# Splitting the first projection of a two-block transformer kernel at half of its features, so that part of it runs between the modulation sums

## The reference

```
mod = silu(c) @ w_mod + b_mod                     # 1024 -> 3 x 1024
shift, scale, gate = split(mod, 3)
h = rms_norm(x, pre_gain) * (1 + scale) + shift   # 512 x 1024
proj = h @ w_in                                   # 1024 -> 3088 columns
```

## Time and profile before

| | us |
|---|---|
| median of 3 runs | 2425.56 |
| profiled execution, device time | 2423.87 |
| its span, first to last instruction | 2422.1 |
| TensorE busy | 2270.7 |
| VectorE busy | 1432.5 |
| ScalarE busy | 962.5 |
| GpSimd busy | 947.6 |
| first matmul of the projection starts | 48.32 |

### The profile page before, as it was taken

How to read it: one execution, slowest core, us unless ns; L and a number is a source line. 1 busy time by engine, 2 the same in 40 slices (tenths; PEclk the granted TensorE clock), 3 DMA queues, 4 the chain that set the end, 5 groups by cost and what they waited for, 6 DMA issues and landing times.

```text
span 2422.1 us, 36259 instructions
## 1 busy us (share of the span) xinstructions
PE 2270.7 (94%) x14374; PEld 1950.2 (81%) x14374; DVE 1432.5 (59%) x2032; ACT 962.5 (40%) x1818; POOL 947.6 (39%) x740
## 2 busy tenths in 40 slices
PE   4998989989998888899999999999999989899998
PEld 4787778877787556689989999898787667799997
DVE  6865647966396644565515235044587764856756
ACT  2335343354425756624211212124325873534433
POOL 3443564435633423326433424235552434221022
PEclk9999999999999999999999999999999999999999
DMA  9550136501252000042313223242430004233232
GB/s 315 181 173 28 29 102 193 158 27 37 70 167 58 1 1 10 1 132 74 118 58 117 79 92 109 61 131 73 158 121 27 1 1 139 87 105 113 88 105 79
DMA packets 164000, 219.13 MB, mean 90 GB/s; under 512 B 19381, under 2 KB 102741, under 8 KB 163705
## 3 DMA queue, kind: packets, MB, share of 16 engines
q1 hardware_dynamic: 163832, 216.82, 28.5%
HBM read 214.69 MB, written 2.10 MB: 90 GB/s over the span
## 4 chain that ended last, share of the span: by engine, by line
PE 57%; DVE 4%; ACT 3%; POOL 2%; issue 2%; DMA 1%; ACTq 0%; DVEq 0%; POOLq 0%; SPq 0%
PE ps L336 14%; PE ps L337 14%; PE ps L338 14%; PE ps L1200 5%; PE ps L1228 4%; PE ps L1250 2%; PE ps L1508 1%; PE ps L1247 1%; PE ps L665 1%; DVE mod_acc_aux L435 1%; POOL h_transposed L653 1%; POOL w_lo L321 1%; PE ps L461 1%; ACT att_probs_two L1293 0%; ACT att_probs_lat L1293 0%
## 5 line engine op out<-in xcount | busy, mean ns | idle before, releaser
L321 POOL TENSOR_TENSOR w_lo<-w_raw,w_hi 128x1024 fp32r<-128x1024 f32 (+3 forms) x205 | 483.9, 2361 | 1010.9 <-ACT w_hi L315 1010.8
L315 ACT ACTIVATE w_hi<-w_raw 128x1024 fp32r<-128x1024 f32 (+3 forms) x232 | 234.4, 1011 | 803.6 <-PE ps L338 731.1
L336 PE MATMUL ps<-w_hi,h_transposed 128*128 128x512 f32 (+3 forms) x1136 | 421.7, 371 | 32.4 <-POOL w_lo L321 15.2
L337 PE MATMUL ps<-w_lo,h_transposed 128*128 128x512 f32 (+3 forms) x1136 | 413.2, 364 | 0.0
L338 PE MATMUL ps<-w_hi,h_transposed 128*128 128x512 f32 (+3 forms) x1136 | 413.0, 364 | 0.0
L336 PE MATMUL ps<-h_transposed,w_hi 128*128 128x384 f32 (+2 forms) x1048 | 337.6, 322 | 7.8 <-POOL h_transposed L653 3.3
L337 PE MATMUL ps<-h_transposed,w_hi 128*128 128x384 f32 (+2 forms) x1048 | 336.6, 321 | 0.0
L338 PE MATMUL ps<-h_transposed,w_lo 128*128 128x384 f32 (+2 forms) x1048 | 336.6, 321 | 0.0
L336 PEld LDWEIGHTS ps<-w_hi,h_transposed 128*128 128x128 f32 x1136 | 218.5, 192 | 72.7 <-POOL w_lo L321 19.6
L337 PEld LDWEIGHTS ps<-w_lo,h_transposed 128*128 128x128 f32 x1136 | 218.7, 192 | 31.5 <-issue 2.2
L338 PEld LDWEIGHTS ps<-w_hi,h_transposed 128*128 128x128 f32 x1136 | 218.5, 192 | 31.6
(11 more groups left out here) (399 smaller groups left out, 4209.7 us busy)
## 6 DMA issues: line engine op xcount, KB each, us to landing
w_raw<-in_ffn_w_in_dram SPq DMA_DIRECT2D x88, 512.0 KB, 3.6
w_raw<-in_ada_w_dram SPq DMA_DIRECT2D x48, 512.0 KB, 3.8
w_raw<-in_ffn_w_out_dram SPq DMA_DIRECT2D x44, 512.0 KB, 3.9
mod_units_one<-in_w_mod_dram SPq DMA_DIRECT2D x80, 256.0 KB, 4.3
w_raw<-in_w_in_dram SPq DMA_DIRECT2D x40, 512.0 KB, 3.8
w_raw<-in_w_out_dram SPq DMA_DIRECT2D x16, 512.0 KB, 3.9
mod_units_one<-in_ada_w_dram SPq DMA_DIRECT2D x32, 256.0 KB, 4.1
mod_unit_even<-in_ada_w_dram SPq DMA_DIRECT2D x16, 512.0 KB, 4.3
```

What stands on the lines that cost most here:

```text
L315: act.activation(split_room(i)[0][:, 0:k * n], src[:, 0:k * n], ACT.Copy).then_inc(w_hi_ready.sem, 1)
L321: eng.tensor_tensor(low, src[:, 0:k * n], high.bitcast(F32), ALU.subtract).then_inc(w_lo_ready.sem, 1)
L336: pe.matmul(acc, left[0], right[0], start=start, stop=False, skip_group_check=shared)
L337: pe.matmul(acc, left[0], right[1], start=False, stop=False, skip_group_check=shared)
```

## The change

- The four modulation jobs are reordered: shift and scale of columns 0-511 come first (jobs 0 and 1), then shift and scale of columns 512-1023 (jobs 2 and 3).
- SyncE loads weight units 0 and 1 of the projection before job 2's blocks, unit 2 before job 3's, and unit 3 after; `first_sp` follows unit 3 instead of unit 1.
- Each tile of X has a semaphore of its own, and squares follow the keeping of job 0 alone. TensorE turns kt 0-3 of X after job 0's turn, then job 1, then kt 4-5.
- ScalarE and GpSimd split units 0 and 1 inside the Modulation phase. The barrier after this phase goes.
- VectorE does kt 0-3 (scale and shift, and now the low parts of the features too, in GpSimd's place) after jobs 0 and 1, then sums jobs 2 and 3, then does kt 4-7. The low part of group g is issued after the scale and shift of group g+2.
- TensorE runs units 0 and 1 of chunk 0, then turns job 2, runs six matmuls of `keep_clock`, turns job 3, turns kt 6-7 of X, and goes on with unit 2. ScalarE keeps job 2, makes the high part of unit 2, keeps job 3, then writes the high parts of kt 4-7.

The core of the diff:

```diff
+                    if i == 2:
+                        for q in range(2):
+                            self.linear.load_unit(sp, 0, q)
+                    if i == 3:
+                        self.linear.load_unit(sp, 0, 2)
...
             def tensor(self, pe):
-                for job in self.jobs[:2]:
-                    job.turn(pe)
+                self.jobs[0].turn(pe)
                 for t in range(XT):
-                    self.norm.turn(pe, t, range(6), None, t == XT - 1)
-                for job in self.jobs[2:]:
-                    job.turn(pe)
+                    self.norm.turn(pe, t, range(4), None, t == XT - 1)
+                self.jobs[1].turn(pe)
+                for t in range(XT):
+                    self.norm.turn(pe, t, (4, 5), None, t == XT - 1)
+
+            def tensor_rest(self, pe):
+                self.jobs[2].turn(pe)
+                self.wait_columns(pe, self.jobs[:2])
+                keep_clock(pe, 6)
+                self.jobs[3].turn(pe)
+                self.wait_columns(pe, self.jobs)
+                for t in range(XT):
+                    self.norm.turn(pe, t, (6, 7), None, t == XT - 1)
...
+                weights_high(act, *self.norm.prime)
+                self.jobs[1].keep(act)
+                weights_high(act, *self.norm.prime)
...
+                    if self.beside and g == len(self.groups) // 2:
+                        self.beside.jobs[2].keep(act)
+                        weights_high(act, *self.prime)
+                        self.beside.jobs[3].keep(act)
...
             def vector(self, dve):
+                half = len(self.groups) // 2
                 for g, (kt, r, tiles) in enumerate(self.groups):
+                    if self.beside and g == 0:
+                        self.beside.wait_columns(dve, self.beside.jobs[:2])
+                    if self.beside and g == half:
+                        for last in (half - 2, half - 1):
+                            self.low(dve, last)
+                        self.beside.vector_rest(dve)
+                        self.beside.wait_columns(dve, self.beside.jobs)
+                    if self.beside and g % half >= 2:
+                        self.low(dve, g - 2)
...
+                linear.other_loads, linear.other_at, linear.loaded, linear.primed = first_sp, 3, 3, 3
+                linear.after_unit = {1: first_modulation.tensor_rest}
```

More of the change, by code:

```diff
@@ L265, in flows @@
                 return phase.residual is not None
-            return isinstance(phase, (NormTransposed, MixTransposed, FirstWeights, Memories)) or (isinstance(phase, Residual) and not phase.last)
+            return isinstance(phase, (NormTransposed, MixTransposed, FirstWeights, Memories, Modulation)) or (isinstance(phase, Residual) and not phase.last)
         def sp_waits_phase(sp, n):
@@ L526, in gpsimd @@
                     self.norm.factor(pool, t)
+                for _ in range(2):
+                    weights_low(pool, *self.norm.prime)
         sq_ready, ms_ready, rstd_ready, scales_ready = (signal(n) for n in ("squares_ready", "meansq_ready", "rstd_ready", "row_scales_ready"))
@@ L540, in wait_bank @@
                 pe.wait_ge(source.bank_signal.sem, source.bank_done[bank])
-        x_landed = signal("x_landed")
+        x_landed = [signal(f"x_landed{t}") for t in range(XT)]
         x_added, y_squared, y_rstd = signal("x_added"), signal("y_squared"), signal("y_rstd_ready")
@@ L611, in scalar @@
             def scalar(self, act):
-                if self.beside:
-                    weights_high(act, *self.prime)
-                elif self.added is None:
+                if self.added is None and not self.beside:
                     for step in range(self.T + 1):
@@ L639, in vector @@
                                       mod_cols[:, self.shift, kt, r:r + 1], ALU.mult, ALU.add).then_inc(ht_full.sem, 1)
+                if self.beside:
+                    for last in (2 * half - 2, 2 * half - 1):
+                        self.low(dve, last)
             def gpsimd(self, pool):
-                if self.added is None and not self.beside:
+                if self.beside:
+                    weights_low(pool, *self.prime)
+                    return
+                if self.added is None:
                     for t in range(self.T):
@@ L648, in gpsimd @@
                         weights_low(pool, *self.prime)
[L649 to L654, removed]
+                    self.low(pool, g)
             def turn(self, pe, t, kts, first, last):
@@ L670, in tensor @@
                 if self.beside:
-                    for t in range(XT):
-                        self.turn(pe, t, (6, 7), None, t == XT - 1)
                     return
@@ L847, in wait_copied, with load_unit @@
                 eng.wait_ge(acc_free.sem, self.f0 + sum(len(t) for _, _, t in self.chunks[:c + 1]))
+            def load_unit(self, sp, c, q):
+                c0, n, _ = self.chunks[c]
+                k = self.units[c][0]
+                row = q if self.row_blocks is None else self.row_blocks[q]
+                weights_load(sp, self.w[row * k * P:(row + 1) * k * P, c0:c0 + n], k, n)
             def sync(self, sp):
@@ L855, in sync @@
                     for q in range(units):
-                        row = q if self.row_blocks is None else self.row_blocks[q]
-                        weights_load(sp, self.w[row * k * P:(row + 1) * k * P, c0:c0 + n], k, n)
+                        if c or q >= self.loaded:
+                            self.load_unit(sp, c, q)
                         if c == 0 and q == self.other_at and self.other_loads:
@@ L878, in scalar @@
                     for q in range(units):
-                        if c or q >= 2:
+                        if c or q >= self.primed:
                             weights_high(act, k, n)
@@ L3415, in load_x @@
             for t in range(XT):
-                sp.dma_start(X[:, t, :], a["x"][0, t * P:(t + 1) * P, :]).then_inc(x_landed.sem, 16)
-        schedule.append(Modulation(mods_one(0, [(0, "shift", None, [0]), (1, "scale", a["pre_norm_gain"][0], [1])], BothRooms(rooms_one[0])), load_x))
+                sp.dma_start(X[:, t, :], a["x"][0, t * P:(t + 1) * P, :]).then_inc(x_landed[t].sem, 16)
+        first_modulation = Modulation([ModJob(a["w_mod"][0], a["b_mod"][0], kind, gain, [(0, 0)], [n], half, n * D + half * HALF, mod_acc_aux,
+                                              BothRooms(rooms_one[0]))
+                                       for half in range(2) for n, kind, gain in ((0, "shift", None), (1, "scale", a["pre_norm_gain"][0]))], load_x)
+        schedule.append(first_modulation)
         for l in range(DEPTH):
```

36 lines of the change are left out of this document (24 added, 12 removed).

## The result

The kernel after takes 2430.97 us (median of 20 runs, 2424.22 to 2438.27), the kernel before, run beside it, 2425.12 us (20 runs, 2420.14 to 2434.29). The ratio is 1.0024, 95% interval [1.0016, 1.0032]: 5.8 us slower, between 3.9 and 7.8. I had forecast 2426.8 us in a range of 2420.5 to 2432.5, with 0.69 for no change that can be told and 0.19 for slower. The range held the time; the likeliest case did not: it said +1.2 us, and its own span was -1 to +4. That the range held is in part luck: it reached up to 2432.5 for rival B, low clock over units 0 and 1, which did not come.

The account below looks back on a forecast made before the run. TensorE is busy nearly throughout, but at job 5's turn VectorE decides by half a microsecond. The turn's +1.15 us, carried to the end, gives 2425.56 + 1.2 = 2426.8 us, range 2420.5 to 2432.5.

Parts of the forecast that it names:

- rival B: TensorE's clock low over units 0 and 1, delaying VectorE's second columns 6 to 8 us: 2433 to 2435 us, chance 0.12.
- the likeliest case: The forecast itself: job 5's turn about 1.2 us later, carried to the end; -1 to +4 us, chance 0.62.
- Steps 1 to 5: Start up to job 4: VectorE has first columns at 29.3, second columns at 54.9, and starts job 4 at 61.4.
- Rival A: VectorE is held less by GpSimd and isn't the bound: 2421.3 us, or 2419 with one more hold gone; chance 0.18.
- Step 5: Second half on VectorE: eight instructions, 5.9 us, and 0.6 more; job 4 starts at 61.4 against 55.10 before.
- Step 6: VectorE from job 4's start to job 5's end: 37.5 us with six GpSimd weight low parts, job 5 summed at 98.9.
- Step 7: TensorE ends chunk 0 4.5 us earlier, idles 2.6 to 4 us, waits some 2 us for job 5; turn +1.15 us.
- Rival C: Job 3's third block late, or low clock in chunk 1 after the idle stretch: 2429 to 2431 us, chance 0.08.
- One sign that I had named: Chunk 1 on TensorE starting before 73 would show that VectorE isn't the bound and the early start's gain stays.
- the sign at job 5's turn: TensorE waiting there for VectorE, summed at 98 to 100, supports the forecast; VectorE already done would show it wrong.
- step 8: Costs nothing: the barrier's going, `first_sp` behind unit 3 (tables land by 56, wanted at 72), new semaphores.

Follow-up runs that it names:

- Experiments 2 and 4: Kernel before with 11 more VectorE instructions before job 5: +8.7 us; kernel after with feature low parts on GpSimd again: +4.4 us; both against kernel before.
- experiment 3: Kernel after with twelve more `keep_clock` calls on TensorE just before job 5's turn: +6.3 us against the kernel before.
- experiment 1: Both kernels with jobs turned behind the third unit of the next chunk: kernel after -1.5 us, kernel before -0.7 us, against the kernel before.
- experiment 5: Kernel after with feature low parts on GpSimd and jobs turned behind the next chunk's third unit: 0.9983, again 0.9972; also without `keep_clock`: 0.9971 of kernel before.

## Why the prediction was right or wrong

Right in its frame: the time at which job 5 is summed and turned is what the change is worth. The steps, with what the two traces of the kernel after have:

| step | forecast | measured | second trace |
|---|---|---|---|
| 1 first columns at VectorE | 29.3 | 27.90 | 28.1 |
| 2 first low part ends, held | 33.8 | 32.2 | 32.4 |
| 2 first half ends | 37.5 | 35.7 | 35.9 |
| 4 unit 1 ends on TensorE | 47.2 | 45.2 | 44.1 |
| 3, 4 job 3 summed | 52.8 | 51.9 | 52.3 |
| 4 second columns | 54.9 | 53.3 | 54.5 |
| 5 job 4 starts | 61.4 | 60.15 | 61.38 |
| 7 job 4 summed | 72.5 | 71.2 | 72.4 |
| 7 chunk 1 starts | 75 | 72.0 | 73.8 |
| 7 chunk 1 ends | 97 | 94.4 | 97.2 |
| 6 job 5 summed | 98.9 | 100.07 | 99.2 |

Steps 1 to 5 were right in mechanism, and my instants lie 1 to 2 us behind those of the first trace. From a job's sums to its columns it took 1.35 us instead of the 2.1 I had read at the end of Modulation, where there was the barrier and TensorE's turn took 1.78 us; here the turns of jobs 1 to 3 took 0.95 to 1.05 us. My 2.1 was a figure at low clock: in the second trace of the kernel before the turn took 1.05 us and the way 1.39. Unit 2's low part (47.39) did meet job 3's sums, for 2.0 us (two took 3.50 instead of 1.54). Rival A, fewer holds, did not come; rival B, low clock over all of units 0 and 1, neither: it was low for 3.4 us from 33 on, as long as I had taken, and in the second trace not at all there. Step 5 sets VectorE's idle time at 7.7 us, where the waits and holds of steps 1 to 5 add up to about 8.5; measured were 4.7 us of waits and 4.0 of holds. Its instants don't hang on this figure.

Step 6 failed by a term in the first trace. From job 4's start to job 5's end I had 37.5 us; it took 39.9. VectorE's own work was as counted within 0.4 us, but GpSimd held it seven times, not six: the seventh is unit 9's low part at 97.16, 2.0 us. I had stopped counting at unit 8 since in the kernel before unit 9's comes behind job 5, and did not ask what a TensorE that is ahead of VectorE sets free. Experiments 2 and 4 show a hold at the same place, behind waits of 6.27 and 5.72 us. In the second trace, with a wait of 2.12 us, the seventh hold did not come: from job 4's start to job 5's end it took 37.8 us with six holds, as forecast. There the low clock from 52 on moved the second columns from 53.3 to 54.5, where I had them with my 2.1 us, and from there to job 5 all came within about 1 us of the forecast. So the late turn is in both traces; the seventh hold is in one.

Step 7 failed by size, in the direction that hides itself (first trace). Chunk 0's end was nearly right, but job 4 was summed at 71.2, TensorE went on at 72.0 and reached the next wait at 94.4: 5.75 us of idle time there instead of 2 (2.12 in the second trace). An earlier TensorE was not a gain, it was a longer wait, and a longer wait had a price that step 7 leaves out: the low clock at the turn of job 5 (98 to 105, and from 99.8 on for 3.4 us in the second trace), 1.6 to 2.1 us by experiment 3. This term, which the sum has at nothing, is missed in both traces. Rival C had this mechanism with 1.6 to 5 us, but put it behind the shorter wait at chunk 0's end, where it came in the second trace only.

One sign that I had named misled: a chunk 1 that starts before 73 was to mean that VectorE isn't the bound. It started at 72.00 and then waited 5.75 us for VectorE. An early chunk 1 only made the next wait longer; the sign at job 5's turn was the one that counted.

Together: +1.15 forecast at job 5's turn, +2.3 measured (2.7 in the second pair, where the kernel after turned 0.9 us earlier and the kernel before 1.2), and some 2 us of clock behind it: 4.4 us at the transposes (4.3 in the second pair), and 3.9 to 7.8 in the time. What step 8 puts at nothing cost nothing by the traces: L435 didn't wait for DMA in jobs 2, 3 or 4, and the tables were there when `first_dve` wanted them.

**What stays open.** Behind 200 us the stretches of low clock lie differently from trace to trace of one kernel: the two traces of the kernel before have 79 and 109 us of low clock in all and spans of 2422.1 and 2426.5; those of the kernel after 98 and 109, and 2429.6 and 2431.7. So a single pair of traces can't say how much of what a start gains or loses reaches the end. For the version of experiment 1 there is a gap: 4.5 us before the mean of the two traces of the kernel before at the mark, but only 1.5 us in the time, at most 3.6. The versions of experiment 5 have none that stands out: 4.8, 5.3 and 7.9 us at the mark, 4.1, 6.8 and 7.0 in the time. Whether the gap is chance or whether something in the later phases takes part of a gain back was not settled. Nor was it tested by itself how much of the loss the seventh hold makes.

## What to carry to other kernels

Before an engine's start is pulled forward, find the next place where it meets another engine, and read which of the two comes later and by how much; here it was VectorE, by 0.5 us, 50 us behind the edit. When the engine that is pulled forward waits, count three things: the wait, the clock that falls behind it, and the work of third engines (here GpSimd's splitting, in one of two traces) that its progress sets free to disturb the one that is late. Take a second trace before a single hold or a single stretch of low clock is named as the cause: here both traces lose the same at the mark by different ways. And ask whether the wait need be there at all: placing the turn of the sums one chunk later was worth 8.2 to 9.5 us at the mark to the changed kernel and 0.5 to 1.8 us to the unchanged one.

## What the runs showed of the hardware that I had not expected

TensorE's granted clock fell behind a wait of 5.75 us (and of 6.27 and 5.72 us), and did not behind one of 2.52 us in the same trace; but in the second trace of the same kernel it fell for 3.4 us behind each of two waits of 2.50 and 2.12 us. 24 short matmuls (as the trace counts them) in the long wait kept it up; twelve between the turns of jobs 2 and 3 did not keep it from falling at 52 to 53 in the kernel after, and in experiment 5 were not needed for it (1.00 with and without them) and cost VectorE 1.8 us of waiting. Subtractions of VectorE from SBUF were held by GpSimd's just as its sums are: 2.75 us against 0.68. That is as the rule of the Trainium skill cited in the prediction (SBUF — State Buffer, section "SBUF: two separate sides") has it.
